# Low parts of the attention queries computed on GpSimd, modulation weights loaded ahead of queries and keys, normalisation and value products at other steps

## The reference

```python
mod = silu(c) @ ada_w + ada_b                      # six vectors of 1024
sh1, sc1, g1, sh2, sc2, g2 = split(mod)
h = rms_norm(x, norm_attn_g) * (1 + sc1) + sh1
q_d, k_d, v_d, iq, ik, iw, q_f, k_f, v_f, f = split(h @ w_in)
o_d = softmax over the selected keys (q_d . k_d / 8) @ v_d      # 8 heads
o_f = softmax(q_f . k_f / 8 + cum_q - cum_k, causal) @ v_f      # 8 heads
y = concat(rms_norm(o_d), rms_norm(o_f))
x = x + g1 * (y @ w_out)
h = rms_norm(x, norm_ffn_g) * (1 + sc2) + sh2
x = x + g2 * ((silu(h @ w_gate) * (h @ w_up)) @ w_down)
return rms_norm(x, final_norm_g)
```

## Time and profile before

| | |
|---|---|
| median of 3 runs | 1405.43 us (1403.14 to 1406.23) |
| the profiled execution | 1403.13 us, its span 1401.4 us |
| PE busy | 1317.3 us, 94% of the span |
| DVE busy | 1023.6 us, 73% |
| POOL busy | 805.2 us, 57% |
| ACT busy | 695.9 us, 50% |
| chain that ended last | PE 76%, DVE 8%, issue 4%, DMA 4% |
| granted TensorE clock, mean | 0.99 |

### The profile page before, as it was taken

How to read it: one execution, slowest core, us unless ns; L and a number is a source line. 1 busy time by engine, 2 the same in 40 slices (tenths; PEclk the granted TensorE clock), 3 DMA queues, 4 the chain that set the end, 5 groups by cost and what they waited for, 6 DMA issues and landing times.

```text
span 1401.4 us, 19481 instructions
## 1 busy us (share of the span) xinstructions
PE 1317.3 (94%) x6595; PEld 1073.5 (77%) x6595; DVE 1023.6 (73%) x1599; ACT 695.9 (50%) x1396; POOL 805.2 (57%) x536
## 2 busy tenths in 40 slices
PE   1999999999898899899999899999999999999996
PEld 0988788888776666667888688888888888788885
DVE  4463779999787888895559777655556666579998
ACT  5623346563486667774435334344443333454545
POOL 0251302323258322651007899888899894798985
PEclk9999999999999999999999999999999999999999
DMA  9131312341524766623210233333332334998883
GB/s 383 48 98 53 98 59 77 106 139 68 143 70 140 227 202 206 188 94 127 99 45 31 76 98 116 111 112 113 113 105 91 113 120 143 362 373 293 274 272 137
DMA packets 130379, 200.53 MB, mean 143 GB/s; under 512 B 10637, under 2 KB 65093, under 8 KB 129258
## 3 DMA queue, kind: packets, MB, share of 16 engines
q1 hardware_dynamic: 130282, 199.30, 42.3%
HBM read 156.99 MB, written 42.27 MB: 142 GB/s over the span
## 4 chain that ended last, share of the span: by engine, by line
PE 76%; DVE 8%; issue 4%; DMA 4%; ACT 3%; POOL 2%; SPq 2%; DVEq 0%; ACTq 0%; POOLq 0%
PE PS L2153 21%; PE PS L2155 21%; PE PS L2154 21%; PE PS L2313 3%; PE PS L2359 3%; PE PS L2332 2%; DMA ada<-in_ada_w_dram 2%; DVE LP L1798 2%; DMA adax<-in_ada_w_dram 1%; DVE AS L2019 1%; POOL WSf L1006 1%; PE PS L2334 1%; DMA rawb<-in_w_down_dram 1%; PE PS L2337 1%; DVE mod L1813 1%
## 5 line engine op out<-in xcount | busy, mean ns | idle before, releaser
L1018 POOL TENSOR_TENSOR WS<-WSf,WS 128x512 fp32r<-128x512 f32 x109 | 161.6, 1489 | 9.1 <-ACT WS L1324 9.1
L1324 ACT CAST WS<-WSf 128x512 fp32r<-128x512 f32 x110 | 68.5, 623 | 196.4 <-POOL WSf L1006 195.7
L1006 POOL TENSOR_TENSOR WSf<-rawg 128x512 f32<-128x512 f32 x55 | 78.2, 1423 | 115.6 <-PE PS L2155 111.3
L2153 PE MATMUL PS<-yh,WS 128*128 128x512 f32 (+2 forms) x360 | 139.0, 386 | 1.5 <-DVE yl L1933 1.5
L2155 PE MATMUL PS<-yh,WS 128*128 128x512 f32 (+2 forms) x360 | 138.7, 385 | 0.0
L2154 PE MATMUL PS<-yl,WS 128*128 128x512 f32 (+2 forms) x360 | 138.7, 385 | 0.0
L2153 PE MATMUL PS<-BS,AS 128*128 128x512 f32 x308 | 120.9, 393 | 5.7 <-DVE BS L2024 3.9
L1245 ACT ACTIVATE LP<-LP,nmin 128x128 f32<-128x128 f32 (+7 forms) x128 | 100.0, 782 | 48.7 <-DVE nmin L1798 47.3
L2155 PE MATMUL PS<-BS,AS 128*128 128x512 f32 x308 | 120.5, 391 | 0.0
L2154 PE MATMUL PS<-BS,AS 128*128 128x512 f32 x308 | 120.4, 391 | 0.0
L2019 DVE TENSOR_TENSOR AS<-rawa,AS 128x512 fp32r<-128x512 f32 x77 | 101.3, 1334 | 25.1 <-ACT AS L1383 24.9
(11 more groups left out here) (337 smaller groups left out, 3850.8 us busy)
## 6 DMA issues: line engine op xcount, KB each, us to landing
rawb<-in_w_down_dram SPq DMA_DIRECT2D x132, 256.0 KB, 4.7
rawa<-gu_scratch SPq DMA_DIRECT2D x77, 256.0 KB, 4.8
gu_scratch<-GS SPq DMA_DIRECT2D x55, 256.0 KB, 4.8
raw<-in_w_in_dram SPq DMA_DIRECT2D x24, 512.0 KB, 3.9
rawg<-in_w_gate_dram SPq DMA_DIRECT2D x22, 512.0 KB, 4.3
rawu<-in_w_up_dram SPq DMA_DIRECT2D x22, 512.0 KB, 4.2
ada<-in_ada_w_dram SPq DMA_DIRECT2D x8, 1024.0 KB, 15.3
qk_scratch<-stage SPq DMA_DIRECT2D x32, 256.0 KB, 2.2
```

What stands on the lines that cost most here:

```text
L1006: pool.tensor_tensor(WSf[m % N_SLOT][:], left(i, mat, a), left(i, mat, b), ALU.add if sign > 0 else ALU.subtract).then_inc(ws_sum, 1)
L1018: pool.tensor_tensor(lo, WSf[m % N_SLOT][:] if b else left(i, mat, a), hi.bitcast(F32), ALU.subtract).then_inc(ws_ready, 1)
L2153: pe.matmul(dst, left[0], right[0], start=first, stop=False)
```

## The change

The low part of the queries is no longer made by VectorE in step 4 (and for head 0 before the stage) but by GpSimd at the end of `prepare`, behind the keys' low part, with a wait for that and one for itself. SyncE, from its iteration 5 on, issues the modulation weights that steps 1 and 2 of the next head need before it waits for and issues the next queries and keys. The normalisation of a pair's two halves goes from ahead of the bias pass of steps 23 and 27 to behind that of steps 20 and 26 (of the pair). One value product goes from step 14 to 15, and three of step 18 go from place 0 to place 1.

```diff
-VALUE_PARTS = {(12, 2): 2, (14, 1): 1, (15, 2): 3, (17, 0): 2, (18, 0): 3, (22, 1): 5, (23, 2): 4}
+VALUE_PARTS = {(12, 2): 2, (15, 2): 4, (17, 0): 2, (18, 1): 3, (22, 1): 5, (23, 2): 4}
-NORM_AT = {PAIR * p + at: (p, half) for p in range(N_PAIR) for half, at in enumerate((23, 27))}
+NORM_AT = {PAIR * p + at: (p, half) for p in range(N_PAIR) for half, at in enumerate((20, 26))}
...
# SyncE
+                while hd >= 5 and n_mod < sum(h * TT + t <= (hd + 1) * TT + 3 for h, t in MOD_AT):
+                    load_mod(n_mod)
+                    n_mod += 1
                 load_qk(hd + 2)
...
# GpSimd, end of prepare
                 pool.tensor_tensor(low, Kd[rows, :], KA[i][rows, :].bitcast(F32), ALU.subtract).then_inc(k_lo, 1)
+                pool.wait_ge(k_lo, hd + 1)
+                pool.tensor_tensor(QT[i][DH:P, :], Qd[DH:P, :], QT[i][DH:P, :].bitcast(F32), ALU.subtract).then_inc(q_lo, 1)
+                pool.wait_ge(q_lo, hd + 1)
...
# VectorE
-            def query_lo(hd):
-                q = QT[0 if hd == 0 else 2 - hd % 2]
-                dve.wait_ge(qk_hi, 2 * hd + 2)
-                dve.tensor_tensor(q[DH:P, :], Qd[DH:P, :], q[DH:P, :].bitcast(F32), ALU.subtract).then_inc(q_lo, 1)
...
-            query_lo(0)
             advance(CHOICE_EARLY)
...
+                biased(s)
                 if s in NORM_AT:
                     normalise(*NORM_AT[s])
-                biased(s)
-                if t == 4 and hd + 1 < 2 * NH:
-                    query_lo(hd + 1)
```

## The result

The kernel after takes 1386.97 us in the median of 4 runs (1386.66 to 1390.48), the kernel before in the same comparison 1404.29 (1402.85 to 1406.23): ratio 0.9878, 95% interval 0.986 to 0.9896. That is 17.3 us faster, in the direction of the forecast and at the fast end of its range (1386 to 1405), but almost twice its 9 us and faster than the band that was given the highest chance (1389 to 1402). The profiled execution took 1386.66 us with a span of 1384.7, 16.7 less than before.

A forecast was written before the change was run, and what follows sets the result against it. TensorE's waits in the attention stage, mostly behind VectorE's bias pass, were taken to bound it. Terms 4.5 + 4.6 + 2.5 + 0.5 = 12.1, three quarters let through, 9 us: about 1396 us, range 1386 to 1405.

The forecast's parts named there:

- the band that was given the highest chance: Whole kernel: the forecast's main outcome, 1389 to 1402 us, chance 0.56.
- What bounds: Attention stage: TensorE's order bounds it, at most 25.1 us of its idle time to be had; gains reach the end.
- Low parts leave VectorE, 4.5: Attention stage: removing 15 VectorE instructions, 30.7 us busy, saves 4.5 of the 5.3 us that reached TensorE.
- Modulation, 4.6 us of stalls and 2.5 of clock: Heads 6 to 11: weights issued earlier save 4.6 of 9.2 us TensorE idle, plus 2.5 us of clock dips.
- the stretch from pass 1 to pass 3: Heads 6 to 11, step 1 to step 3 bias pass: from 6.2 to some 5.4 us, 0.8 less per head.
- GpSimd's window shifts by 0 to 3 us toward the head's start: Modulation heads: GpSimd's window starts at or just ahead of step 0, so sums meet its casts or subtractions.
- One and a half of four dips: Heads 6, 7, 9 and 11: one and a half of four TensorE clock dips go, 2.5 us.
- Three quarters: Sum of terms: removed waits uncover others, so three quarters of 12.1 us come through, 9 us.
- Normalisation 0.5, values 0: Attention stage: moved normalisation gains 0.5 us; moved value products gain 0, bounds minus 1 to plus 1 us.
- All stalls go: Rival: sums run before GpSimd's subtractions, all 9.2 + 5.3 and three or four dips vanish, 20 us: 1385; chance 0.18.
- Excluded sums: Rival, heads 6 to 11: both modulation sums meet GpSimd's subtractions; net 7 us slower, 1412; chance 0.12.
- Covered: Rival: VectorE's waits give way to ScalarE's and dips stay, 0 to 3 us gained, 1404; chance 0.14.

The follow-up runs named there:

- e10: Kernel before plus modulation weights issued ahead and queries' low parts on GpSimd, normalisation and values as before: 1388.05 us, ratio 0.9861.
- e2: Kernel before with only the modulation weights of steps 1 and 2 issued ahead of the next queries and keys: 1392.83 us, ratio 0.992.
- e1: Kernel before with only the low parts of the queries moved to GpSimd: 1406.56 us, ratio 1.0002.
- e13: Kernel after with the next keys' load issued ahead of the queries', each waiting for its own low part only: 1384.69 us, ratio 0.9856.
- e9: Kernel after with a second pair of buffers for the raw queries and keys of heads 9 and 11: 1391.06 us, ratio 0.9884.
- e3: Kernel after with the queries' low parts back on VectorE in step 4: 1400.56 us, ratio 0.9966 to the kernel before.
- e11: Kernel before plus modulation weights issued ahead and the normalisation's new place, low parts on VectorE, values as before: 1394.67 us, ratio 0.9914.
- e14: Kernel after with the queries' low parts of heads 0 to 6 back on VectorE, the others on GpSimd: 1397.42 us, ratio 0.993.
- e17: Kernel after with the keys' load issued first, run beside the unchanged kernel after on the same chip: 1385.80 us, ratio 0.9871 to before.
- e16: Kernel after, unchanged, run again as partner of the keys-first kernel on the same chip: 1389.26 us, ratio 0.988 to before.
- e7: Kernel after with the normalisation back at steps 23 and 27 ahead of the bias pass: 1387.28 us, ratio 0.9875 to before.
- e8: Kernel after with the value products at their old places: 1390.00 us, ratio 0.9894 to before.

## Why the prediction was right and wrong

**What bounds.** Right: the stage gave 17.0 of the 17.3 us by the profiles, and what stands behind it moved along unchanged. TensorE's idle time in the stage fell from 25.0 to 14.3 us, its busy time by 6.3. Nearly all of the busy time's part lies in heads 6 to 11. Outside them the busy time stayed the same although two dips of the clock, 3.4 us, are new there; why is open.

**Low parts leave VectorE, 4.5.** Right in size. Outside heads 6 to 11, heads 0 to 5 give 3.6, head 12 gives 2.7 and head 15 1.1, and heads 13 and 14 take 2.8 back, of which 1.7 is the new dip of the clock in head 13: 4.6. The better measure is e10 less e2, which differ in the low parts alone: 4.6 us from the first bias pass to the last (245.5 and 250.1), 4.8 in the medians, and 8 by the ratios to the kernel before. The forecast costed the later load at nothing worth naming. It had looked at GpSimd's own queue behind `prepare`, and at modulation loads standing in front of queries and keys, but not at what stood behind the load on SyncE when the low part let it go late. In e1 head 6 gave back everything the part had gained. The change as a whole escapes it only because its second part takes the weights out of that queue.

**Modulation, 4.6 us of stalls and 2.5 of clock: this is the step that failed.** In heads 6 to 11 it measured 6.3 and 5.4, 12 in place of 7. The term that was mis-sized is the stretch from pass 1 to pass 3: 5.4 us in the forecast, 0.8 less per head, and 4.3 in the mean after, 1.8 less. It rested on one sentence, that "GpSimd's window shifts by 0 to 3 us toward the head's start", so that both sums would meet its subtractions. Two things were wrong with it.

First, the window went the other way, 5 to 6 us into heads 7 and 8 and still 3 into head 11, so that in heads 7 to 10 no sum was held at all. The forecast had the terms of the turn right (`prepare` 7 to 10 us, landing 7) but added them to a start at the head's start. In the kernel before, VectorE tied the turn to the head: the load went out at the end of L1749 in step 4, 10.3 us into head 8, and landed with the next head. With the low part on GpSimd that tie is gone. The turn of load, landing and `prepare` releases itself, every 14 to 16 us, and `prepare` already starts 5.9 and 5.7 us into heads 4 and 5. Why it settles at that place is not shown.

Second, even near the head's start the meeting costs less than the forecast took. In e2 the window stayed there, and the stretch took 4.6 us in the mean: the first sum arrives before GpSimd has come to its subtraction, and the one that arrives second is the one that is held. The Trainium skill states it so (SBUF — State Buffer, "Who interferes with whom"): "Issue order, not op shape, decides who blocks." The rows agree in both directions: the sum of 3.19 us in e13 and the subtraction of 3.23 in e9. The forecast quoted the rule for both directions and priced only one, as a loss on VectorE.

How much of the gain is the weights and how much the place? The weights alone gave 12.0 us in these heads (e2), as much as the whole change, so they carry it. But place has a price of 1 to 2 us in a head where it is bad (e1, e3, e11, e14, e17). In the kernel before, heads 7 and 11 had their weights in time too. There the second sum was held (2.86 and 2.93 us, the first of these in the earlier trace rows), and TensorE's two longest waits, 1.93 and 2.15 us, stand behind it.

**The clock.** One and a half of four dips were to go. In heads 6 to 11 all four went (1.00 from 459 to 547) and one new dip came at the start of head 6; over the whole stage it was one dip less, since heads 0 and 13 have one each. Dips were counted as if they went in proportion to the stalls. The four that went stood behind waits of 1.35 to 2.15 us, and those waits went. But a dip does not follow from its wait alone: 1.46 us had none in the kernel before, and the 0.95 us in head 0 that both kernels have is followed by one only in the kernel after. The amount of this half is in part luck: the second profile of the kernel after (e16) loses 3.4 us to the clock in heads 6 to 11 and not 1.7.

**Three quarters.** The sum was cut from 12.1 to 9 for waits that would come up behind. With the terms at their measured size, 4.6 + 6.3 + 5.4 + 0 is 16.3 of a measured 16.7 in span, so this second term failed too: no such cut can be seen. What came up behind, the waits named "issue" of 3.5 us, is already in the terms. No row says three quarters.

**Normalisation 0.5, values 0.** Right together with the low parts, within the intervals (e7, e8, e10). Not right in general: beside low parts on VectorE the same two moves cost 6 to 8 us (e3).

**The rivals.** *All stalls go* (1385, given 0.18) was nearest, and its own sign, a stage shorter than 245 us, came true (243.5). Its reason, sums ahead of the subtractions, is what heads 7 to 10 of the kernel after show. *Excluded sums* needs a sum to arrive second; in the kernel after that happened at most once in heads 7 to 11 (2.02 us in head 11), but e1, e3, e11, e14 and e17 have it in two or more heads each at 1 to 2 us, so it was a real danger that the shifted window avoided and the forecast did not foresee. *Covered* would have been true of the low parts alone in its number (e1), not in its reason, which was ScalarE.

## What to carry to other kernels

When a step is moved between engines, follow what waits for it and then what stands behind that waiter in its queue: a load released 3 us later into its head was harmless by itself, but VectorE's wait for the load issued behind it grew from 2.7 to 7.6 us. Of two parts that were worth 0 and 11 us by themselves the pair was worth 16 or more (e10), so a part that measures zero alone should be read stretch by stretch before it is dropped. Where two engines exclude each other, ask who arrives first: making the critical one's data early carried most of the gain here. Then look where its second instruction falls, since a sum that came just behind the start of a subtraction still cost 1 to 2 us.

## What the runs showed that was not expected

- GpSimd's copies are held by VectorE's sums as well as its subtractions are. The forecast gave a copy beside a sum no price. In head 9 of e13 the sum from 499.23 ends at 500.61, and the copy below ends at 501.50 and not at 500.50:

```profile
499.46 2.04 POOL L923 CAST KA<-Kd 128x1024 fp32r<-128x1024 f32 x1
```

- The same kernel's runs spread more in some orders than in others: e14's ten runs go from 1385.47 to 1399.13, e13's five from 1384.05 to 1386.34.
